# The last mixing norm: mean subtracted before the root, the norm's factor on a diagonal in the transposing products, the gain row as a column in the copies

## The reference

```python
def layer_norm(v, g, b):  # end of the second layer
    y = (v - mean(v)) / sqrt(var(v) + 1e-5) * g + b
x = layer_norm(ALPHA * x + (1.0 + g2) * y, ln_g[l, 1], ln_b[l, 1])

h = _rmsnorm(x, g_mix[i])        # xf * rsqrt(mean(xf * xf) + EPS) * g
z = h @ w_in[i]                  # 1024 x 2048
conv_v, conv_g, lru_x, lru_g = jnp.split(z, ...)
...                              # convolution, recurrence, output product
hf = _rmsnorm(x, g_ffn[i])       # routing, 32 experts of 1024 x 512
e = _rmsnorm(p[i] @ w_ple[i], g_ple_proj[i])
x = x + sigmoid(_rmsnorm(x, g_ple[i]) @ w_ple_gate[i]) * e
```

## Time and profile before

| | us |
|---|---|
| three timed runs | 1248.54, 1251.73, 1254.90 |
| their median | 1251.73 |
| the profiled execution | 1250.06 |
| its span | 1248.3 |
| TensorE busy in the span | 1201.6 |
| VectorE busy | 674.9 |
| ScalarE busy | 496.1 |

### The profile page before, as it was taken

How to read it: one execution, slowest core, us unless ns; L and a number is a source line. 1 busy time by engine, 2 the same in 40 slices (tenths; PEclk the granted TensorE clock), 3 DMA queues, 4 the chain that set the end, 5 groups by cost and what they waited for, 6 DMA issues and landing times.

```text
span 1248.3 us, 16544 instructions
## 1 busy us (share of the span) xinstructions
PE 1201.6 (96%) x6589; PEld 828.2 (66%) x6589; DVE 674.9 (54%) x1213; ACT 496.1 (40%) x745; POOL 54.1 (4%) x104
## 2 busy tenths in 40 slices
PE   6999899999999999999999999999999999999997
PEld 2697688887789868888878786445444444554446
DVE  5589969887779786765468475211111121121126
ACT  1478654444565575444445374111111111111126
POOL 0100101000000000001001200000000000000000
PEclk9999999999999999999999999999999999999999
DMA  9997858888646554856555769999999999999991
GB/s 367 389 329 279 311 219 325 330 312 322 256 162 240 182 223 169 319 194 226 178 221 208 244 253 417 426 425 424 426 427 424 427 426 427 426 426 425 425 420 42
DMA packets 49979, 395.50 MB, mean 317 GB/s; under 512 B 6561, under 2 KB 8801, under 8 KB 11394
## 3 DMA queue, kind: packets, MB, share of 16 engines
q1 hardware_dynamic: 38466, 337.17, 67.3%
q0 software_dynamic: 9216, 54.45, 12.1%
q10 hardware_dynamic: 2240, 3.10, 1.0%
HBM read 391.20 MB, written 3.49 MB: 316 GB/s over the span
## 4 chain that ended last, share of the span: by engine, by line
PE 81%; DVE 8%; DMA 6%; ACT 3%; issue 1%; SPq 1%; ACTq 0%; DVEq 0%
PE psum L1326 17%; PE psum L747 10%; PE psum L750 10%; PE psum L754 10%; PE psum L1367 8%; PE psum L1257 4%; DMA slabs<-in_w 3%; PE psum L802 2%; PE psum L806 2%; PE psum L804 2%; PE psum L1265 2%; DMA staged<-in_ada 2%; DVE w_parts L2060 1%; DVE aring L2043 1%; PE psum L1024 1%; PE psum L1036 1%
## 5 line engine op out<-in xcount | busy, mean ns | idle before, releaser
L2060 DVE TENSOR_TENSOR w_parts<-w_raw,w_parts 128x2048 fp32r<-128x2048 f32 x106 | 241.7, 2288 | 75.2 <-ACT w_parts L1457 75.1
L1457 ACT ACTIVATE w_parts<-w_raw 128x2048 fp32r<-128x2048 f32 x106 | 202.0, 1911 | 79.0 <-DMA w_raw<-in_units 79.0
L1326 PE MATMUL psum<-slabs,arena 128*64 128x512 f32 x896 | 223.0, 593 | 1.7 <-issue 1.3
L747 PE MATMUL psum<-w_parts,h_parts 128*128 128x512 f32 x416 | 166.1, 399 | 2.2 <-ACT h_parts L1457 1.3
L750 PE MATMUL psum<-w_parts,h_parts 128*128 128x512 f32 x416 | 163.4, 393 | 0.0
L1326 PEld LDWEIGHTS psum<-slabs,arena 128*64 128x64 f32 x896 | 73.2, 137 | 110.9 <-issue 109.4
L1457 ACT ACTIVATE arena<-psum 128x512 f32<-128x512 f32 (+1 forms) x43 | 23.8, 557 | 251.3 <-PE psum L1340 140.8
L754 PE MATMUL psum<-w_parts,h_parts 128*128 128x512 f32 x416 | 111.7, 390 | 0.6 <-DVE h_parts L2237 0.6
L2043 DVE CUSTOM_DVE_ANT_0 aring<-aring,cb 128x1024 f32<-128x1024 f32 x80 | 94.5, 1218 | 2.8 <-DMA aring<-in_ada 2.7
L747 PEld LDWEIGHTS psum<-w_parts,h_parts 128*128 128x128 f32 x416 | 79.0, 190 | 19.5 <-DVE act_tm L2256 1.4
L754 PEld LDWEIGHTS psum<-w_parts,h_parts 128*128 128x128 f32 x416 | 77.9, 188 | 17.8 <-DVE h_parts L2237 1.2
(11 more groups left out here) (330 smaller groups left out, 1874.8 us busy)
## 6 DMA issues: line engine op xcount, KB each, us to landing
w_raw<-in_units SPq DMA_DIRECT2D x110, 1024.0 KB, 5.0
slabs<-in_w SPq DMA_DIRECT2D x30, 2048.0 KB, 18.1
slabs<-in_w SPq DMA_DIRECT2D x52, 1024.0 KB, 16.4
aring<-in_ada POOLq DMA_DIRECT2D x40, 1024.0 KB, 5.2
arena<-in_w SPq DMA_DIRECT2D x16, 2048.0 KB, 18.9
w_odd<-in_w SPq DMA_DIRECT2D x16, 2048.0 KB, 21.0
w_odd<-in_w SPq DMA_DIRECT2D x16, 1024.0 KB, 19.4
staged<-in_ada SPq DMA_DIRECT2D x8, 1024.0 KB, 18.8
```

The source lines that it names most:

```text
L747: mm(psum[:, bank, :], high(tile, tok), w_hi(k)[:, col:col + 512], start=first and bank not in begun, stop=False, skip_group_check=True)
L1326: ins = nc.tensor.matmul(psum[s * CAP:(s + 1) * CAP, w, :], xe_t[:, kt, s * CAP:(s + 1) * CAP], up_weights(w, s, b, kt), start=kt == 0, st ...
L1457: return nc.scalar.activation(out_ap, in_ap, func, **kw)
L2060: v.tensor_tensor(w_lo(k), raw(k), w_hi(k).bitcast(F32), ALU.subtract).then_inc(w_split, 1)
```

## The change

The mean is now subtracted before the root is waited for: the first pass of `last_norm` waits only for the moments, and the reciprocal follows it. The passes of `mixed(t)` that multiplied the rows by the token's factor and the gain row are gone. In their place ScalarE multiplies the identity by the token factors (`mix_diag`, 128x128), and TensorE, instead of transposing normed rows, multiplies the stream `x_tm` by this diagonal as a plain f32 product, which transposes and scales in one. The gain `g_mix` comes as a column for each feature tile (`V("g_mix", kt)`, part of the vectors loaded at the start): `mix_highs` is eight copies of 128x128 with a scale for each partition instead of two of 128x512, and `mixed_low` eight passes of 128x128 (bank times gain, less the high part) instead of two of 128x512. `z_unit(0)` waits for each copy of tile 1 by itself. The row `mix_row` and its load are gone. VectorE's order is changed: the reciprocal for tile 0 stands between the two halves of tile 1's residual, the reciprocal for tile 1 between the low parts of tile 0.

```diff
-VECS = [("g_ple", KT), ("g_ffn", KT), ("b_ada", 96), ("ln_g", 32), ("ln_b", 32), ("subln_g", 1),
+VECS = [("g_ple", KT), ("g_ffn", KT), ("g_mix", KT), ("b_ada", 96), ("ln_g", 32), ("ln_b", 32), ("subln_g", 1),
-        mix_row = arena2[:, 2184:3208]
+        mix_diag = arena2[:, 2184:2440].rearrange("p (t n) -> p t n", t=TT)
@@ def h_event(q, t, c):
-            return KT + 4 * q + 2 * t + c + 1
+            return KT + 4 * (q if q < 3 else q - 1) + 2 * t + c + 1
@@ GpSimd
-            gain_row(mix_row, "g_mix", early_rows)
             gain_row(proj_row, "g_ple_proj", early_rows)
@@ TensorE
+            def mixed_tiles(t):
+                pe.wait_ge(normed, 12 + t + 1)
+                for c in range(2):
+                    if t:
+                        pe.wait_ge(h_low, low_event(3, 0, c))
+                    for k in range(4):
+                        ins = nc.tensor.matmul(psum[:, 6 + c, k * P:(k + 1) * P], x_tm[:, t, (4 * c + k) * P:(4 * c + k + 1) * P],
+                                               mix_diag[:, t, :], start=True, stop=True)
                     ins.then_inc(normed_t, 1)
@@ def z_unit(j, between=(None, None)):
-                        if kt % 4 == 0:
-                            pe.wait_ge(h_high, h_event(3, 1, kt // 4))
+                        pe.wait_ge(mix_high, KT + kt + 1)
@@
-            pe.wait_ge(early_rows, 48)
+            pe.wait_ge(early_rows, 32)
             pe.wait_ge(gated, 44)
             embedding(0, 4)
-            normed_tiles(3, 0)
+            mixed_tiles(0)
             pe.wait_ge(moments_ready, 8)
             embedding(1, 2)
-            normed_tiles(3, 1)
+            mixed_tiles(1)
@@ ScalarE
+            def mix_diagonal(t):
+                act.wait_ge(rms_ready, rms_no("mix", t))
+                A(mix_diag[:, t, :], ident, Cp, scale=rms_of("mix", t, 3)).then_inc(normed, 1)
+
             def mix_highs(t):
-                for c in range(2):
-                    act.wait_ge(normed_t, 12 + 2 * t + c + 1)
-                    A(h_hi[:, 4 * c:4 * c + 4, t * P:(t + 1) * P], by_k(6 + c), Cp).then_inc(h_high, 1)
+                for kt in range(KT):
+                    if kt % 4 == 0:
+                        act.wait_ge(normed_t, 12 + 2 * t + kt // 4 + 1)
+                    A(h_hi[:, kt, t * P:(t + 1) * P], psum[:, 6 + kt // 4, kt % 4 * P:(kt % 4 + 1) * P], Cp,
+                      scale=V("g_mix", kt)).then_inc(mix_high, 1)
 
             ln_deviation(3, 0)
             mix_square(0)
+            mix_diagonal(0)
             ln_deviation(3, 1)
             mix_highs(0)
             mix_square(1)
+            mix_diagonal(1)
             mix_highs(1)
@@ VectorE
             def last_norm(t):
+                if t == 0:
+                    dve.wait_ge(rows_in, 64)
+                dve.wait_ge(moments_ready, 6 + t + 1)
+                for c in cols:
+                    ins = stt(resid[:, t, c], resid[:, t, c], moments[:, t, 0:1], ln_rows[:, 0, c], ALU.subtract, ALU.mult)
+                    ins.then_inc(dve_seq, 1)
+                at_ = seq[0]
+                seq[0] += 2
                 dve.wait_ge(ln_std, 6 + t + 1)
                 link(v.reciprocal(moments[:, t, 3:4], moments[:, t, 2:3]))
                 for n, c in enumerate(cols):
                     dve.wait_ge(dve_seq, at_ + n + 1)
                     stt(x_tm[:, t, c], resid[:, t, c], moments[:, t, 3:4], ln_rows[:, 1, c], ALU.mult,
                         ALU.add).then_inc(x_ready, 1)
-            def mixed(t):
-                root("mix", t)
-                dve.wait_ge(x_ready, 2 * t + 2)
-                if t == 0:
-                    dve.wait_ge(early_rows, 48)
-                for c in cols:
-                    stt(resid[:, t, c], x_tm[:, t, c], rms_of("mix", t, 3), mix_row[:, c], ALU.mult,
-                        ALU.mult).then_inc(normed, 1)
-            def mixed_low(t):
-                for c in range(2):
-                    dve.wait_ge(h_high, h_event(3, t, c))
-                    tiles = (slice(None), slice(4 * c, 4 * c + 4), slice(t * P, (t + 1) * P))
-                    v.tensor_tensor(h_lo[tiles], psum[:, 6 + c, :].rearrange("p (k t) -> p k t", t=P),
-                                    h_hi[tiles].bitcast(F32), ALU.subtract).then_inc(h_low, 1)
+            def mixed_low(t, c):
+                dve.wait_ge(mix_high, KT * t + 4 * c + 4)
+                for kt in range(4 * c, 4 * c + 4):
+                    tok = slice(t * P, (t + 1) * P)
+                    ins = stt(h_lo[:, kt, tok], psum[:, 6 + c, kt % 4 * P:(kt % 4 + 1) * P], V("g_mix", kt),
+                              h_hi[:, kt, tok].bitcast(F32), ALU.mult, ALU.subtract)
+                ins.then_inc(h_low, 1)
 
             ln_residual(3, 0)
             last_norm(0)
-            ln_residual(3, 1)
-            mixed(0)
+            ln_half(3, 1, 0)
+            root("mix", 0)
+            ln_half(3, 1, 1)
             last_norm(1)
-            mixed_low(0)
-            mixed(1)
-            mixed_low(1)
+            mixed_low(0, 0)
+            root("mix", 1)
+            mixed_low(0, 1)
+            for c in range(2):
+                mixed_low(1, c)
             split(Z_AT + 1)
             split(Z_AT + 2)
@@ def embedding_scaled(t):
                 root("ple_proj", t)
+                if t == 0:
+                    dve.wait_ge(early_rows, 32)
```

More of the change, by code:

```diff
@@ L383, in build @@
         early_rows, late_rows = sem("early_rows"), sem("late_rows")
+        mix_high = sem("mix_high")
         e_out = sem("e_out")
@@ L455, in h_event, with low_event @@
         def h_event(q, t, c):
+            return KT + 4 * (q if q < 3 else q - 1) + 2 * t + c + 1
+        def low_event(q, t, c):
             return KT + 4 * q + 2 * t + c + 1
@@ L924, in normed_tiles @@
                     pe.wait_ge(normed, 4 * q + 2 * t + c + 1)
-                    if t and q < 3:
+                    if t:
                         pe.wait_ge(ln_whole, 4 * q + c + 1)
-                    elif t:
-                        pe.wait_ge(h_low, h_event(3, 0, c))
                     for k in range(4):
@@ L1021, in z_unit @@
                     if j == 0 and kt % 4 == 0:
-                        pe.wait_ge(h_low, h_event(3, 1, kt // 4))
+                        pe.wait_ge(h_low, low_event(3, 1, kt // 4))
                     for s in range(2):
@@ L1402, in gate_high @@
                            stop=False, skip_group_check=True)
-                pe.wait_ge(h_low, h_event(4, t, j // 2))
+                pe.wait_ge(h_low, low_event(4, t, j // 2))
                 for s in range(2):
@@ L2006, in _ @@
             act.wait_ge(rms_ready, rms_no("final", 0))
-            act.wait_ge(normed, 18)
+            act.wait_ge(normed, 16)
             for c in range(2):
@@ L2959, in lay_out @@
     vecs = {
[L2960 removed]
+        "g_ple": cols(f["g_ple_2"]), "g_ffn": cols(f["g_ffn_2"]), "g_mix": cols(f["g_mix_2"]), "b_ada": cols(f["b_ada"]), "ln_g": cols(f["ln_g"]), "ln_b": cols(f["ln_b"]), "subln_g": cols(f["diff_subln_g"]),
         "conv_b": cols(f["conv_dw_b_2"]), "conv_ln_g": cols(f["conv_ln_g_2"]), "conv_ln_b": cols(f["conv_ln_b_2"]),
```

10 lines of the change are left out of this document (2 added, 8 removed).

## The result

| | before | after |
|---|---|---|
| median of 16 runs, alternating on one chip | 1250.07 us | 1253.49 us |
| lowest and highest | 1248.46, 1254.90 | 1251.91, 1256.52 |
| ratio, 95% interval | | 1.0023 [1.0015, 1.0032] |
| profiled execution, its span | 1250.06, 1248.3 | 1256.52, 1254.7 |

By the ratio the kernel is 0.23% slower, 2.9 us, with an interval of 1.9 to 4.0; the two medians differ by 3.4. The forecast was 1.0 us faster. The time lies inside the range; the sign is wrong.

A forecast was written before the change was run, and what follows sets the result against it. TensorE, busy 96% of the span, bounds the kernel, late on with the saturated weight stream. The norm's serial chain shortens by 1.0 us: 1249.1 against the profiled 1250.06, or 1250.7 against the median 1251.73; range 1246.5 to 1254.7.

The forecast's parts named there:

- The terms of the norm: Timetable of the norm between second layer and mixing products: first mixing product at 662.68 instead of 663.68, 1.0 us earlier.
- tile 0's copies: ScalarE's eight gain copies of 128x128 at the norm, spaced 0.257 us, from 656.6 to 658.76.
- diagonal: Tile 1's diagonal at the norm: one ScalarE operation replacing two gain passes, taken as 0.38 us.
- four low passes: VectorE's low part of tile 0 at the norm: 0.265 us per following pass, bounds 0.2 and 0.345.
- subtracting first: Mean ahead of the root at the norm: subtracting passes cover the wait for ScalarE's root, about 0.3 us in tile 0.
- rival A: Chance 0.16: at the norm, products with the diagonal go as fast as transposes (0.11 us); 1.65 us gained, 1250.1.
- The covers that were counted: Behind the norm: ScalarE neither ahead nor behind; TensorE has 0.9 us to spare at the second mixing unit, 0.5 at the third.
- rival B: Chance 0.14: TensorE waits the gain out at the second or third mixing unit, or the stream doesn't move; 1251.7, no change.
- C: Chance 0.09: at the norm, gain copies don't overlap and cost 0.455 us each; 1.3 us slower, 1253.0.
- D: Chance 0.03: at the norm, a plain product costs four transposes, 0.44 us each; 2.4 us slower, 1254.1.
- Is the cover still there behind the seam?: Step on the mixing units behind the norm: spare times of 0.9 and 0.5 us hold; start can move at most about 1.5.
- Does the microsecond reach the end?: Step on the expert weight stream, saturated near 749 us: it shifts with TensorE, so all of the 1.0 us is taken.

The follow-up runs named there:

- Before with the late write: The kernel before, with two idle VectorE fills (768 and 256 columns) ahead of the first convolution input, so its write goes out later; ratio 1.0015.
- fixed kernels: After with the load held until the write landed (0.9994), small VectorE operations moved behind the third convolution input (1.0003), or the load held until the copies landed (0.9996).
- the one with both fixes: After with the first convolution input early and the weight load held until the first write has landed; 1249.07 against before's 1250.50 us, ratio 0.9988.
- filled kernel: After with four plain f32 products put on TensorE ahead of its wait for the first convolution's copies; ratio 1.0020 to before.

## Why the prediction was wrong

*The terms of the norm held.* Mixing was to start 1.0 earlier; it did by 1.12. In distances from the residual: stream's first subtracting pass at 4.83 by the forecast, 4.80 measured; the stream whole 7.76, 7.73; tile 0's copies 5.79, 5.69, in 2.16, 2.18; sum of squares 7.85, 7.77; diagonal 0.38, 0.40; sixteen records of tile 0 0.11 apart (1.78/16); four low passes 1.15, 1.12 (the 0.265 taken between 0.2 and 0.345, now (2.16 - 1.12)/4 = 0.26); first mixing product 11.87, 11.75. The worth of subtracting first was put at about 0.3, measured 0.33. The products' surplus over transposes, 0.65 as the difference between the forecast and rival A, measured 0.61.

*The covers that were counted held.* ScalarE's next job was to start neither earlier nor later: 13.16 against 13.29. The second unit's split ends at 16.67 (forecast 16.8), the third's starts at 16.98 (17.06), and TensorE reaches the third unit 0.46 after its bank is free (677.66 against 677.20; forecast 0.5). Neither of rival B's two waits appeared. C and D fell with the spacing of 0.26 and the factor of two. The prediction also held that timing can tell 0.5% from no change; sixteen runs of each kernel told 0.23%, with an interval of under 0.1% to either side.

*The step that failed* is "Is the cover still there behind the seam?", with the sentence under "Does the microsecond reach the end?" on which it leaned: "in SyncE's program each load ahead of that stands behind a wait for a mixing unit, a convolution or an output product, so the stream shifts with TensorE". The loads do shift so, and that is the cause of the loss. The prediction followed ScalarE, VectorE and TensorE's banks, and let the transfers shift as one stream. But two engines issue transfers there. SyncE's loads shift with TensorE. GpSimd's write and copies for the first convolution follow VectorE, which stands there behind the split that, in the prediction's own words, "waits for ScalarE and stays where it was". What hangs on one moved by 1.1 against the other. Both rows were in the trace of before: the load at 675.46, 1.08 behind the write at 674.38. The forecast shift of 1.0 would have brought them to within 0.1.

*How much cover there was.* In after the copies take 7.2 from the first issue (29.74) to their landing (36.93). By that figure they were in at 26.52 + 7.2 = 33.7 before, some 2.3 ahead of the convolution at 36.07; that is an estimate, since no wait shows their landing there and the copies of after may themselves be slower than before's. The change cut the cover from two sides: TensorE came 1.1 earlier and the copies 3.2 later, 4.3 in all, of which 2.3 were covered and 2.0 are the wait. Before with the late write gives the cover once more: its copies went out 4.1 later and TensorE waited 2.1, so 2.0 were covered. The 1.7 of half clock comes on top.

*What the rivals missed.* The slower side was given 0.09 and 0.03 at C and D, both at the norm, where every price was known from rows. The place where no price was known, a small transfer through memory beside a large load, had no rival. B came nearest ("the stream doesn't move with it") but forecast no change: the stream did move, and that cost more than it gave.

How sure is the cause? The meeting is shown from both sides: taken out of after by moving the load or the write, and put into before by moving the write alone. Not shown is what happens inside the transfers. The Trainium skill ("DMA: Bandwidth & Descriptors", Queues, rings and completion order) says that each DMA engine takes turns between its queues by whole packets; the same page (Latency and other measured facts) puts HBM access at 0.2 us on average and 2 us under high load. Both fit a write that loses some 3 us when 1 MB is issued beside it. No run here tells them apart. Why a load issued 1 us behind the write does so little isn't shown either; the write takes only 2.5 where no load is near, so by then part of it may be over.

The timed ratios of the fixed kernels (0.9994, 1.0003, 0.9996) have intervals that hold both no change at all and a gain of 1.1 us, the middle one only at its edge; of the fixed kernels that compute everything only the one with both fixes has an interval that leaves 1 out. That the change's own gain goes through rests on the traces, three of which show the routing products 1.1 earlier and the end 0.9 to 1.4 earlier than before, and on that one ratio. That the half clock is worth 1.7 rests on traces too: the timed runs of the filled kernel, 1.0020, don't show it. Of the three traces with filling products two still have the 1.7 at the end (598.7 and 598.5 against after's 600.4) and one has lost 1.0 of it; why is open.

## What to carry to other kernels

When a change moves one engine and not another, list what each of them releases on every DMA queue, and look for a small transfer with a consumer waiting beside a large one with none: their distance changes by the full shift, and here 1 us of shift cost 3 us. The remedy is cheap where small work can be taken out from ahead of the small transfer's producer, or where the large load can be made to wait for the write alone; hold it longer than that and it falls on the next small one. And compare two traces by distances from a point just ahead of the change, since their starts differed by more (3.5 us) than the effect.

## What the runs showed of the hardware

- A write of 143.5 KB to memory, issued by GpSimd, took 2.5 to 3.2 us to the next issue that waits for it, 5.5 to 6.4 when a load of 1 MB on SyncE's queue was issued within 0.25 us of it, and 3.5 with the load 0.4 behind. The second of these writes took 6.3 with a load issued 4.1 ahead of it and one 1.7 behind, and 3.5 with none issued in the 11 us ahead of it and one 2.6 behind.
- After 2.0 and 2.1 us without work TensorE ran part of the next convolution at half its clock in one kernel and, after 2.1, all of it at the full one in another (5.35 against 3.66 for the same 64 products), each in two traces of two. After 1.73 to 1.76 us without work in the routing it ran part of the following products at half its clock in thirteen traces of sixteen and all of them at the full one in three (4.7 to 5.5 against 3.84).
- A plain f32 product of 128 by 128 costs 0.223 us and a transpose of the same size 0.11, at this seam as among the experts.
- A ScalarE copy of 128x128 out of PSUM with a scale for each partition follows the one ahead at 0.26 us although one alone shows 0.36 or more; the diagonal, a single one, took 0.40.
